# Two-layer transformer kernel: the second layer's first eight projection slots as seven products instead of eight, in three rotating PSUM banks

## What is computed

```
h  = rmsnorm(x,  norm1_g[l]) * (1.0 + sc1)  + sh1        # 512 tokens
hc = rmsnorm(xc, norm1_g[l]) * (1.0 + sc1c) + sh1c       # 256 context tokens
p, pc = h @ w_in[l], hc @ w_in[l]     # 1024 -> 7 * 512 + 32 gate columns
# cuts of 512: q, k, v, o of the mLSTM heads, then q, k, v of the neighbourhood attention, then gates
x = x + g1 * (y @ w_out[l]);  then the MLP.  xc is updated only where need_ctx (first layer)
```

## Time and profile before

| what | value |
|---|---|
| median of 3 runs | 3449.39 us (3446.28 to 3449.89) |
| the profiled execution | 3450.99 us, its span 3449.4 us |
| mean granted TensorE clock | 0.990 of 2.4 GHz |
| PE busy | 3327.8 us, 96% of the span |
| DVE, ACT, POOL busy | 58%, 21%, 30% |
| DMA | 301.70 MB, mean 87 GB/s |
| second layer, slots 0 to 7 | from 1176.79 us to 1396.93 us after the span's start |

### The profile page before, as it was taken

The page is one execution under the profiler, slowest core; times in us unless marked ns, Lnnn a source line. Parts: engine busy times, 40 slices in busy tenths (PEclk is TensorE's granted clock), DMA queues, the critical chain, the costliest instruction groups (busy, mean ns, idle before and its releaser), DMA issues. The chain is left out here.

```text
span 3449.4 us, 39911 instructions
## 1 busy us (share of the span) xinstructions
PE 3327.8 (96%) x15432; PEld 2474.5 (72%) x15432; DVE 2005.4 (58%) x3518; ACT 719.7 (21%) x1548; POOL 1031.7 (30%) x800
## 2 busy tenths in 40 slices
PE   5999999999999999999999999999999998999998
PEld 4567775555555556778888854888886885688887
DVE  7666377666766443267545656654444786665543
ACT  2243231100000224131111124111111233311110
POOL 0110223333233000224444401444441550244443
PEclk9999999999999999999999999999999999999999
DMA  6332321333331121231222221222222220022222
GB/s 259 107 115 80 105 67 49 123 119 112 122 110 61 61 70 51 68 92 62 86 87 86 87 84 61 86 86 86 86 98 86 80 84 28 26 75 91 91 86 86
DMA packets 63580, 301.70 MB, mean 87 GB/s; under 512 B 7232, under 2 KB 19648, under 8 KB 37280
## 3 DMA queue, kind: packets, MB, share of 16 engines
q1 hardware_dynamic: 51872, 260.87, 22.5%
q0 software_dynamic: 6528, 18.75, 1.7%
q10 hardware_dynamic: 4992, 19.53, 1.6%
HBM read 294.27 MB, written 2.88 MB: 86 GB/s over the span
## 5 line engine op out<-in xcount | busy, mean ns | idle before, releaser
L2590 POOL TENSOR_TENSOR scratch<-ring 128x512 f32<-128x512 f32 (+1 forms) x160 | 224.2, 1401 | 1527.6 <-PE psum L694 1116.6
L694 PE MATMUL psum<-big,scratch 128*128 128x256 f32 (+1 forms) x2240 | 607.6, 427 | 4.8 <-DVE big L2025 4.8
L694 PEld LDWEIGHTS psum<-big,scratch 128*128 128x128 f32 x2240 | 426.0, 190 | 169.6 <-issue 8.2
L694 PE MATMUL psum<-H,scratch 128*128 128x256 f32 (+1 forms) x2144 | 500.7, 389 | 3.6 <-ACT cb L1352 3.6
L694 PEld LDWEIGHTS psum<-H,scratch 128*128 128x128 f32 x2144 | 405.9, 190 | 84.0 <-ACT cb L1352 8.9
L665 PE MATMUL psum<-H,ring 128*128 128x512 f32 x928 | 423.1, 607 | 13.4 <-ACT H L1434 11.5
L694 PE MATMUL psum<-big,ring 128*128 128x256 f32 (+1 forms) x1584 | 426.0, 422 | 8.7 <-issue 3.2
L694 PE MATMUL psum<-H,ring 128*128 128x256 f32 (+1 forms) x1536 | 402.9, 407 | 8.3 <-ACT H L1434 4.2
L694 PEld LDWEIGHTS psum<-big,ring 128*128 128x128 f32 x1584 | 303.0, 192 | 115.3 <-issue 5.3
L694 PEld LDWEIGHTS psum<-H,ring 128*128 128x128 f32 x1536 | 297.6, 195 | 83.4 <-issue 9.1
L665 PEld LDWEIGHTS psum<-H,ring 128*128 128x128 f32 x928 | 175.1, 194 | 221.7 <-issue 216.4
(11 more groups left out here) (361 smaller groups left out, 4133.7 us busy)
## 6 DMA issues: line engine op xcount, KB each, us to landing
ring<-in_wall SPq DMA_DIRECT2D x202, 1024.0 KB, 4.9
big<-in_wada SPq DMA_DIRECT2D x48, 512.0 KB, 3.6
big<-in_wada POOLq DMA_DIRECT2D x32, 512.0 KB, 3.8
big<-in_wada ACTq DMA_DIRECT2D x4, 2048.0 KB, 20.4
scratch<-in_rpb ACTq DMA_DIRECT2D x16, 512.0 KB, 4.5
X<-in_xin SPq DMA_DIRECT2D x4, 768.0 KB, 11.8
scratch<-negd SPq DMA_DIRECT2D x8, 384.0 KB, 8.3
big<-negd SPq DMA_DIRECT2D x8, 384.0 KB, 9.3
```

The costliest lines, as they stand in the source:

```text
L694: mm = pe.matmul(fast_bank(st, q, b), lhsT, rhs(k), start=start and k == 0, stop=k == kt - 1, skip_group_check=True)
L2590: pool.tensor_tensor(s1, a21, a22, ALU.add).then_inc(combo_own, 1)
```

## The change

The second layer's slots 0 to 7 (50 to 57 of the ring) become a stage `BLOCK` of `fast_stage`. The eight parts of it:

- PE makes 28 matmuls a slot over 384 tokens (256 in the query slots 0 and 3) in place of 32 over 512 and 256. The banks rotate within 0, 1 and 2, so each slot's products wait for the drains of the slot before (`c11_done`, `c12_done`, `c21_done`), as in `HEADS`. The four points of a slot now come after products 2, 6, 7 (which has product 1 of the next slot behind it) and 4. The gate matmuls come after slot 0's second product.
- POOL combines the weights of the eight slots, into a part of `big` and into `cb`. The masks of the bias tables, until now added as they arrived, come after slots 4, 6 and 7.
- DVE makes the 16 input combinations, writes them over `X`, and adds three of four quarters of every slot (`to_block`); two of a slot's additions are in two pieces, since attention wants its columns in another order.
- ACT copies three partial products and the fourth quarter.
- The gate work of DVE is cut in four: `gate_sizes` and `gate_series` in slot 0, `gate_scans` at the end of slot 1, `gate_peaks` in slot 2 between the first and the second addition.
- `X` of the 512 tokens (2 MB) is sent to DRAM (`kept`) at ring slots 50 to 52, and read back at slot 60. Both directions are on SP's queue, between the ring's loads.
- `mix_input(Y[1])` waits for the data read back.
- All later stages keep their form; their counts move by eight slots.

```diff
@@ Stage, tables
+        if self.kind == "block":
+            return [("block", 0, s) for s in range(8)]
+BLOCK = Stage("block", True, 50, 36, 2, 0, 16, -1, 1, 8)
+STAGES = [Y[0], MLP[0], BLOCK, Y[1], MLP[1], YA, SW0, HEADS, YB, SW1]
...
+        combos_block = [a.rearrange("p (i k c) -> p i k c", i=4, k=4) for a in (B_[:, 0:2048], cb[:])]
...
         def h_mix(st, i, j):
+            if st is BLOCK:
+                return X_[:, (4 * i + j) * 384:(4 * i + j + 1) * 384]
...
         def fast_bank(st, q, i):
-            if st is HEADS:
-                return bank(((0, 1, 2), (2, 0, 1), (1, 2, 0))[(q - st.q0) % 3][i], st.width())
+            if st is HEADS or st is BLOCK:
+                turn = (q - st.q0 + (st is BLOCK)) % 3
+                return bank(((0, 1, 2), (2, 0, 1), (1, 2, 0))[turn][i], width_at(st, q))
@@ block.sync
+                if 50 <= n <= 52:
+                    for i in range(n - 50, n - 49 if n < 52 else 4):
+                        sp.wait_ge(c21_done, FAST[46 + i] + 1)
+                        sp.dma_start(kept[:, 2 * i:2 * i + 2], X[:, 2 * i:2 * i + 2, CTX:TOK]).then_inc(x_in[i], 16)
+                if n == 60:
+                    for i in range(4):
+                        sp.wait_ge(x_in[i], 32)
+                        sp.dma_start(X[:, 2 * i:2 * i + 2, CTX:TOK], kept[:, 2 * i:2 * i + 2]).then_inc(x_in[i], 16)
@@ block.tensor
-                for s in range(14):
+                def between_blocks(x, i):
+                    if x == 0 and i == 2:
+                        gates(1)
+                    mixer_point(1, 4 * x + (2, 6, 7, 4).index(i))
+                if l:
+                    fast_stage(BLOCK, between=between_blocks)
+                    pe.wait_ge(c21_done, w.fast)
+                for s in range(8 * l, 14):
@@ block.scalar, fast_stage
+                    if kind == "block":
+                        mixer_point(1, 4 * x + 2)
+                        act.wait_ge(prod[4], q + 1)
+                        for dst, of in block_parts(s, 1, 0):
+                            ins = act.activation(dst, of(fast_bank(st, q, 1)), ACT.Copy,
+                                                 scale=HD ** -0.5 if queries(st, q) else 1.0)
+                        ins.then_inc(c21_done, 1)
+                        mixer_point(1, 4 * x + 3)
@@ block.vector, fast_stage
+                def to_block(q, s):
+                    def took(i, f, a, done, also):
...
+                        for dst, of in block_parts(s, f, a):
+                            c, y = of(fast_bank(st, q, b)), of(piece(st, p, q))
...
+                                ins = dve.tensor_tensor(dst, c, y, ALU.add)
+                        ins.then_inc(done, 1)
+                    took(2, 0, 0, c11_done, 1)
+                    if s == 0:
+                        gate_sizes(1)
+                    if s == 2:
+                        gate_peaks()
+                    for pt in (4 * s, 4 * s + 1):
+                        if pt >= NA_FIRST:
+                            mixer_point(1, pt)
+                    took(3, 0, 1, c12_done, 6)
+                    took(7, 1, 1, c22_done, 5)
+                    if s == 0:
+                        gate_series(1)
+                    if s == 1:
+                        gate_scans()
+                    for pt in (4 * s + 2, 4 * s + 3):
+                        if pt >= NA_FIRST:
+                            mixer_point(1, pt)
@@ block.gpsimd
+                    masks_after_slot = {4: (0, 1, 2, 3), 6: (4, 5), 7: (6, 7)}
+                    def block_masks(x):
+                        for h in masks_after_slot.get(x, ()):
+                            add_mask(h)
+                    mix_weights(BLOCK, block_masks)
```

More of the change, by code:

```diff
@@ L464, in build, with combos_of, wait_block @@
         NA_FIRST, KEYS_TURN, STATES, UNITS_FROM = 14, (35, 36, 37), (38, 39, 41, 42), 44
-        def block_unit(l, slot, f):
-            u = LAYER_UNITS * l + 2 * slot + f
-            return u % 2, u // 2 + 1
+        def combos_of(st, q):
+            return (combos_block if st is BLOCK else combos)[q % 2]
+        def wait_block(eng, l, slot, f):
+            if l and slot < 8:
+                eng.wait_ge(c22_done if f else c12_done, BLOCK.q0 + slot + 1)
+                if f:
+                    eng.wait_ge(c21_done, BLOCK.q0 + slot + 1)
+                return
+            u = LAYER_UNITS * l + 2 * (slot - 8 * l) + f
+            eng.wait_ge(acc_free[u % 2], u // 2 + 1)
         def acc(u, n=512):
@@ L682, in fast_stage @@
                 assert (w.fast, w.slot) == (q0, s0)
-                rotated = st is HEADS
+                rotated = st is HEADS or st is BLOCK
                 def product(x, i, b, cols, rhs, start, ready=None):
@@ L748, in fast_stage @@
                         second()
+                        between(x, 2)
                     pe.wait_ge(combos_ready, q + 1)
@@ L1629, in _ @@
                 load_bias(l, 0)
-                for s in range(14):
+                if l:
+                    fast_stage(BLOCK)
+                for s in range(8 * l, 14):
                     for f in range(2):
@@ L2094, in fast_stage @@
                         to_heads(q0 + x, s)
+                    elif kind == "block":
+                        to_block(q0 + x, s)
                     elif kind != "in":
@@ L2411, in _ @@
                     ring_tiles(0, 0, 6, mod_junk[0])
-                gates(l)
                 if ctx_on:
+                    gate_sizes(0)
+                    gate_series(0)
+                    gate_scans()
+                    gate_peaks()
                     ring_tiles(0, 6, 4, mod_junk[0])
-                for pt in range(NA_FIRST, 56):
+                else:
+                    mix_input(BLOCK, block_tile)
+                    fast_stage(BLOCK)
+                for pt in range(NA_FIRST if ctx_on else 32, 56):
                     mixer_point(l, pt)
@@ L2420, in _ @@
                 ln_gate(l, 1)
-                skip(14, 32)
+                skip(14 - 8 * l, 32 - 16 * l)
+                if l:
+                    for g in range(4):
+                        dve.wait_ge(x_in[g], 48)
                 dve.wait_ge(nY, NA0[l + 1])
@@ L2587, in mix_weights @@
                         pool.wait_ge(q_ssq, 1)
-                    if x == 1 and kind == "in":
+                    if x == 1 and kind in ("in", "block"):
                         pool.wait_ge(h_ready, st.h0 + DT)
@@ L2827 @@
     negd = nc.dram_tensor("negd", (4, 32, TOK), F32, kind="Internal").ap()
-    build(nc, out=out, negd=negd, **args)
+    kept = nc.dram_tensor("kept", (P, DT, SEQ), F32, kind="Internal").ap()
+    build(nc, out=out, negd=negd, kept=kept, **args)
     r = run_bass_kernel_spmd(nc, [{f"in_{name}": a for name, a in arrays.items()}], core_ids=[0])
```

110 lines of the change are left out of this document (77 added, 33 removed).

## The result

| | before | changed |
|---|---|---|
| median of 20 runs each | 3447.84 us (3444.24 to 3450.11) | 3453.02 us (3450.16 to 3455.35) |
| the profiled execution | 3450.99 us, span 3449.4 | 3452.9 us, span 3451.0 |
| granted TensorE clock | 0.990 | 0.986 |
| DMA | 301.70 MB | 305.90 MB |

The ratio is 1.0015, 95% interval 1.0009 to 1.0022: 5.2 us more, which a repetition on another occasion confirmed (3452.50 against 3447.01, ratio 1.0014, 1.0006 to 1.0023). The forecast was 3450.0, within 3437 to 3460, with no clear change (under 0.2%) as the likeliest case, and that is how it came out. The forecast change was +0.6 us, though, and the measured one is +5.2.

A forecast was written before the change was run, and what follows sets the result against it. PE, busy 96% of the span, was taken to bound the kernel. The terms -18.8 + 2.2 + 9.0 + 2.1 + 3.5 + 2.6 gave +0.6 us, so a median of 3450.0 us, range 3437 to 3460.

The forecast's parts named there:

- PE's own work: Second layer's slots 0 to 7: block products over 384 or 256 tokens replace 151.3 us of matmuls by 132.5, gaining 18.8.
- Start: Slot 0's products 1 and 2 wait for ACT's shifted tiles of H, losing 4.3 us instead of 2.1: +2.2.
- DRAM: The residual's 2 MB sent out from ring slot 50 and read back behind slot 60 is hidden: 0 us.
- DVE's queue: Slots 0 to 2: gate work between DVE's additions, slowed by POOL, makes PE wait before product 4 of slot 2: +9.0 us.
- the scans' window: After product 7 of slot 1, POOL's four weight operations run beside DVE's gate scans and cost 3.3 us.
- the peaks' window: After product 7 of slot 2, POOL's four weight operations beside DVE's gate peaks cost 3.3 us, its mask 1.0 more.
- Clock behind it: After PE's 9 us wait in slot 2 the granted clock falls to its lower level for some microseconds: +2.1 us.
- Attention at uneven distances: Attention points with one block product between them: PE's turn waits for DVE's extremes and normalising, slowed by POOL: +3.5 us.
- Rotary embedding: At point 28 the values wait for point 27's rotary embedding, ready 5.2 us after the scores, PE after 2.58: +2.6 us.
- DVE getting through: Rival: gate steps and POOL's operations interleave well in slots 0 to 2, queue term 1.0, no clock fall: -12.5, 3437; chance 0.25.
- The masks were late: Rival: bias masks miss the first attention scores, slipping everything behind by 2 to 4 us: 3453; counted within the forecast's 0.56.
- POOL shutting DVE out: Rival: POOL blocks DVE's scans, peaks and normalisings in slots 1 to 7, 4.9 us a window: +10.2, 3460; chance 0.19.

The follow-up runs named there:

- last kernel: Changed kernel with point 27's rotary embedding first, peaks after slot 2's last addition, POOL's slot 3 weights behind the scans, slot 4's behind the peaks: 3433.93 us.
- the last two kernels: Changed kernel with rotary embedding first and POOL's slot 3 and 4 weights behind the peaks (3435.28 us); same with peaks after slot 2's last addition (3433.93 us).
- the run with both windows closed: Changed kernel with POOL combining the weights of slots 3 and 4 only after the peaks: 3437.92 us, ratio 0.9972 to the kernel before.

## Why the prediction was right, and where it was not

- **PE's own work, -18.8**: held. Two block products take 1212.17 - 1207.02 = 5.15 us. In the last kernel, nearly without waits, the stage is 205.5 us; 220.1 - 18.8 + 2.2 for the start, and 1.3 of waits (0.53 and 0.75) at the first turn of the attention, make 204.8.
- **Start, +2.2**: held. Products 1 and 2 took 1182.90 - 1175.11 = 7.8 us (7.7 forecast).
- **DRAM, 0**: held, by the run without it.
- **DVE's queue, +9.0**: 9.26. Place and cause were right, the parts less so. By the runs, 0.35 is the queue order (1.0 forecast), 3.04 the scans' window (3.3; DVE itself lost 3.4 there), 5.87 the peaks' window with its mask (3.3 + 1.0), and the 0.8 us lost on the series were covered (0.4 forecast). The scans' window cost what the rows of the MLP say (3.4), and was spent on the end of the series, not on the scans; the peaks' window cost 4.2 in the copies, between those rows and the 4.9 of `HEADS`, and 1.7 beside the mask. (That 4.9 is 3.9 lost and 1.0 to 1.1 for the neighbour, which took 2.15 us for 1.07 at 2740.49 in the kernel before; "about as much again" says it wrongly.) The Trainium skill's rule (SBUF — State Buffer, "Who interferes with whom") that a VectorE instruction with two SBUF inputs and a GpSimd one shut each other out for a whole instruction fits the rows: the subtraction ended 0.81 us behind the mask, and two of the steps in the scans' window 0.80 us behind one of POOL's operations each (1221.67 and 1223.60, against 1220.87 and 1222.80), so nearly all of their own 0.95 came after it. The four copies have one SBUF input, which the rule as the prediction gives it leaves out; the same section counts copies among the instructions that can contend, and the trace shows it. The estimate by that rule was 15.7, because it let every operation of POOL hold DVE for its full length. In the scans' window the two engines took turns instead, each holding the other: DVE lost 3.4 us, and POOL's four operations took 7.1 instead of 5.1. The reciprocal (4.94 us beside three of them, 4.95 without) was not held up, as was forecast.
- **Clock behind it, +2.1**: 2.2 (4.76 against 2.58).
- **Attention at uneven distances, +3.5**: the waits shown are 0.47 and 0.75 us, 1.2 in all. POOL's window did meet one normalising (1.30 for 0.49 us), and the masks met two more, which were held up by 1.5 and 1.6 us (2.02 at 1303.57, 2.13 at 1335.18), but no wait of PE came of those two. What DVE lost hardly reached PE: over-estimated by some 2 us. The 0.47 came of the first mask arriving late (see the rivals).
- **Rotary embedding, +2.6**: 2.4, but I had written that no wait but the one of 9 us would bring the clock down. That sentence was wrong: 1.6 us more, so 4.0. Of the 2.3 us too many in the attention, this miss takes back 1.4; that is luck.
- The sum with the measured sizes is -18.8 + 2.2 + 9.3 + 2.2 + 1.2 + 4.0 = +0.1; the stage shows +1.1 and +1.3 against the first profile of before. About 1 us remains in pieces that no run separates.
- **What failed**: "Behind slot 7 everything keeps its form, and PE bounds it, so what is gained or lost here arrives at the end." It holds for a delay put into the kernel before, within 0.7 us, but kernels with the new stage come out 2 us later behind it, the changed one nearly 4, and the prediction itself had named that as a sign of being wrong. 0.7 us are the wait in `HEADS` shown above; the rest is in part the clock, and not settled.
- **The level, and luck.** The change was forecast as +0.6 and is +5.2: 4.6 us apart, of which some 0.9 are the stage (+1.5 against the mean of the two profiles of before) and 3.8 what comes behind it. The medians, 3450.0 and 3453.0, are only 3.0 apart because the anchor was too high: three executions of the kernel before had given 3449.4 where twenty give 3447.8. The second error hid 1.6 us of the first.
- **The rivals.** DVE getting through did not happen. The masks were late, but by a third of a microsecond, not 2 to 4: the first extremes waited for POOL's mask, which had itself waited for its transfer, and began 1.65 us behind their scores (1.29 in the last kernel, where the masks were in time), and PE's wait of 0.47 us behind them is gone in that kernel. That this rival's 3453 is the measured time is chance. POOL shutting DVE out was half true: it makes 8.9 of the 9.26 us, but at 3.0 and 5.9 us a window, not 4.9 everywhere. Without it the change is worth 9.5 us, and the stage is 11.6 shorter than before, near the 12.5 under the first rival; the 11.7 and 13.1 of the last two kernels contain the rotary edit too.

## What to carry to other kernels

When small steps are slotted between the operations that release a busy engine, look at what POOL does in those microseconds, and hold POOL back by a wait on work that it has time for: a single semaphore wait at each of two weight combinations turned a loss of 5 us into a gain of 9.5. Tiny copies between SBUF operands are then the costliest of all for their size. A wait of PE costs more than its length where the clock falls behind it: here 2.2 us for 9.3, 1.7 for 3.4, and 1.6 for 2.4. The last is not to be counted on: with an earlier wait gone, the same 2.4 us brought no fall, and removing them gained 2.1 in the stage instead of 3.8. And code that an edit does not touch may still meet another engine a quarter of a microsecond earlier and pay for it.

## What the hardware showed that was not expected

- Four DVE copies of 32 x 6 numbers and less took 1.18 to 1.24 us each beside POOL's 128 x 512 operations, 0.15 to 0.16 with POOL idle.
- Either engine can keep the other out for a whole series. POOL's first weight combination of the new stage took 7.31 us at 1182.48 instead of 1.27, beside DVE's sixteen input combinations, which ran back to back until 1188.66. In `HEADS` one step of DVE took 4.93 or 1.08 us, as the first of POOL's four operations began 0.28 or 0.53 us behind it.
- The clock fell behind short waits too, and not each time: after 2.4 us without work it came behind the wait, when PE had already begun again (1.00 up to 1370, 0.50 from 1372), and in the run with both windows closed it did not come behind the same 2.4 us; after 1.0 us at 1505 it came in the first profiles of both kernels, and in that of the kernel with the peaks behind, while waits of 0.45 to 0.82 us there, in four others, were followed by none.
- The same code, from the turn of `y` to the end, differed by up to 3.5 us from profile to profile of the kernel before with nothing but a delay ahead of it, while medians of 11 runs repeated the delay within 0.7 us. A stage's length is read from one profile, a kernel's surplus of a few microseconds only from medians.
